# Two-layer hybrid trunk: per-block roots and transposed scaled blocks in the prologue

## The reference

```python
def rmsnorm(x, g):
    xf = x.astype(jnp.float32)
    y = xf * lax.rsqrt(jnp.mean(xf * xf, axis=-1, keepdims=True) + EPS)
    return (y * g.astype(jnp.float32)).astype(x.dtype)

def even_mixer(h, cos, sin, w_in, conv_w, q_g, k_g, w_out):
    p = h @ w_in
    sc, q, k, v, iq, ik, iw = jnp.split(p, EVEN_SPLIT, axis=-1)
    ...
    q = apply_partial_rope(rmsnorm(q.reshape(bsz, s_len, ATT_HEADS, HEAD_DIM), q_g), cos, sin)
    ...
    yb = indexed_sparse_attention(q, k, v, iq, ik, iw * IDX_SCALE, topk)
    return jnp.concatenate([ya, yb], axis=-1) @ w_out

for layer in range(DEPTH):
    x = x + even_mixer(rmsnorm(x, ev_norm[i]), ...)      # layer 0; odd_mixer in layer 1
    x = x + conv_ffn(rmsnorm(x, ffn_norm[layer]), ...)
```

## Time and profile before

| | us |
|---|---|
| median of 3 runs | 2179.6 (2179.0 to 2180.37) |
| span of the profiled execution | 2178.9 |
| TensorE busy | 2073.2 |
| VectorE busy | 1394.8 |
| ScalarE busy | 1099.9 |
| GpSimd busy | 1096.4 |

### The profile page before, as it was taken

How to read it: one execution, slowest core, us unless ns; L and a number is a source line. 1 busy time by engine, 2 the same in 40 slices (tenths; PEclk the granted TensorE clock), 3 DMA queues, 4 the chain that set the end, 5 groups by cost and what they waited for, 6 DMA issues and landing times. The chain is left out here.

```text
span 2178.9 us, 29915 instructions
## 1 busy us (share of the span) xinstructions
PE 2073.2 (95%) x11334; PEld 1008.8 (46%) x11334; DVE 1394.8 (64%) x1998; ACT 1099.9 (50%) x1649; POOL 1096.4 (50%) x840
## 2 busy tenths in 40 slices
PE   6989977889999999999999999989999999999998
PEld 3544435654444444444434444555444444444444
DVE  9788888857775575575544036695867467467552
ACT  6459946644664564554323225443566466455520
POOL 6103333315677767756584023503476766765642
PEclk8999988999999999999999999999999999999999
DMA  4002110002112211212232001101211211221212
GB/s 175 20 1 57 32 31 2 14 13 70 49 58 59 68 49 58 59 49 68 66 105 59 0 20 39 46 5 50 57 49 51 66 58 49 68 59 48 59 40 96
DMA packets 186493, 110.20 MB, mean 51 GB/s; under 512 B 4351, under 2 KB 180902, under 8 KB 186358
## 3 DMA queue, kind: packets, MB, share of 16 engines
q1 hardware_dynamic: 185894, 107.00, 16.5%
q0 software_dynamic: 464, 1.39, 0.2%
HBM read 104.18 MB, written 4.19 MB: 50 GB/s over the span
## 5 line engine op out<-in xcount | busy, mean ns | idle before, releaser
L1229 PE MATMUL ps<-arena 128*128 128x512 f16 x2712 | 594.0, 379 | 3.9 <-DVE ps L2751 2.5
L1229 PEld LDWEIGHTS ps<-arena 128*128 128x128 f16 x2712 | 264.9, 98 | 326.2 <-DVE ps L2751 5.5
L1229 PE MATMUL ps<-h_hi,arena 128*128 128x512 f16 x1216 | 372.1, 381 | 4.7 <-DVE arena L2842 4.2
L782 POOL TENSOR_SCALAR w_scaled<-stage 128x1024 f32<-128x1024 f32 (+4 forms) x82 | 79.4, 969 | 587.7 <-PE ps L1088 415.8
L2760 DVE SCALAR_TENSOR_TENSOR work<-ps,fvec,work 128x1023 f32<-128x1023 f32 (+1 forms) x176 | 221.6, 1279 | 21.8 <-ACT work L1966 18.7
L1229 PE MATMUL ps<-h_lo,arena 128*128 128x512 f16 x608 | 231.8, 381 | 0.0
L1229 PEld LDWEIGHTS ps<-h_hi,arena 128*128 128x128 f16 x1216 | 119.4, 98 | 151.8 <-issue 8.2
L1088 PE MATMUL ps<-arena 128*128 128x512 f16 x708 | 156.4, 383 | 14.0 <-DVE xT L2642 11.7
L836 POOL TENSOR_TENSOR w_scaled<-stage 128x512 f32<-128x512 f32 (+2 forms) x62 | 70.0, 1129 | 193.1 <-ACT stage L1697 192.9
L1697 ACT ACTIVATE stage<-stage 128x2048 f32<-128x2048 f32 (+2 forms) x62 | 104.5, 1686 | 111.7 <-DMA stage<-in_ffn_w_up_dram 95.3
L1088 PE MATMUL ps<-h_hi,arena 128*128 128x512 f16 x576 | 150.3, 382 | 1.7 <-ACT small L1869 1.7
(11 more groups left out here) (370 smaller groups left out, 3868.3 us busy)
## 6 DMA issues: line engine op xcount, KB each, us to landing
stage<-in_ffn_w_up_dram SPq DMA_DIRECT2D x84, 512.0 KB, 3.8
stage<-in_ffn_w_down_dram SPq DMA_DIRECT2D x48, 384.0 KB, 3.2
stage<-in_od_w_in_dram SPq DMA_DIRECT2D x20, 512.0 KB, 3.8
stage<-in_ev_w_in_dram SPq DMA_DIRECT2D x12, 512.0 KB, 3.8
arena<-in_x_dram SPq DMA_DIRECT2D x8, 512.0 KB, 6.7
stage<-in_ffn_w_down_dram SPq DMA_DIRECT2D x16, 256.0 KB, 2.7
out_dram<-arena SPq DMA_DIRECT2D x8, 512.0 KB, 3.5
stage<-in_od_w_out_dram SPq DMA_DIRECT2D x12, 256.0 KB, 2.7
```

The source lines that it names most:

```text
L782: nc.gpsimd.tensor_scalar(scaled, src, W_SCALE, 1.0, ALU.mult, ALU.mult).then_inc(w_parts, 1)
L1229: last = mm(ps[:, bank, :], left, b[:, k, :], start=(fresh and k == 0 and pss == 0), stop=(k == nk - 1 and pss == 2), skip_group_check=True)
```

## The change

The squares of a block are followed at once by its own root and reciprocal (`square_tokens`, `token_root`). Blocks 0 to 3: GpSimd multiplies the tokens of a block in place by their root, between two of its angle steps; TensorE turns the scaled blocks a second time, four blocks to a bank (`h_turn`, 8 tiles); ScalarE makes the high half straight from PSUM with the gain as its scale (`first_high`), and VectorE the low half from PSUM (`first_low`). Blocks 4 to 7 keep the norm on VectorE, with steps m of 8 to 15, its product in `h_second` in the arena. Blocks 0 and 1 are projected together: first both halves of h by the weights' high halves for all 8 tiles, then h's high halves by the weights' low halves. VectorE splits weight tiles 0 to 4, GpSimd 5 to 7. The masks stand behind the weight tiles; `conv_vectors` runs at b = 1. The first four blocks of x and the vectors are issued ahead of the other four. An early root on `small` loads ScalarE's table once.

```diff
-        TW_BY_DVE = (0, 1)
-        TW_BY_POOL = (2, 3, 4, 5, 6, 7)
+        TW_BY_DVE = (0, 1, 2, 3, 4)
+        TW_BY_POOL = (5, 6, 7)
...
-            for b in range(NB):
+            def load_x(b):
                 sp.dma_start(x_tok[:, b, :], t["x"][0, b * P:(b + 1) * P, :]).then_inc(x_landed[b], 16)
+            for b in range(NB // 2):
+                load_x(b)
...
                 sp.dma_start(vrows[at[name]:at[name] + VEC_ROWS[name], :], src).then_inc(vec_landed, 16)
+            for b in range(NB // 2, NB):
+                load_x(b)
             for k in range(KT):
...
+            def normalise(b):
+                pool.wait_ge(x_turned, 2 * b + 2)
+                pool.wait_ge(tok_rstd, b + 1)
+                G.tensor_scalar(x_tok[:, b, :], x_tok[:, b, :], rms8[:, b:b + 1], 1.0, ALU.mult, ALU.mult).then_inc(tok_normed, 1)
             for src, dst in ((2, 4), (3, 5)):
+                if src == 3:
+                    for b in range(NB // 2):
+                        normalise(b)
...
-            norm_lows(0)
...
+            def h_turn(m):
+                hf, k = divmod(m, KT)
+                if k == 0:
+                    pe.wait_ge(tok_normed, NB // 2)
+                if m == 2:
+                    pe.wait_ge(rope_act, 1)
+                if m == 3:
+                    pe.wait_ge(vec_ready, 1)
+                if m >= 4:
+                    pe.wait_ge(h_ready, m - 3)
+                for j in range(4):
+                    last = tr(ps[:, 4 + m % 4, j * P:(j + 1) * P], x_tok[:, 4 * hf + j, k * P:(k + 1) * P], ident[:])
+                last.then_inc(hf_ready, 1)
+            for b in range(6):
+                x_turn(b)
             pe.wait_ge(vec_landed, 16 * 6)
-            tr(ps[:, 5, 0:NVEC], vrows[0:NVEC, :], ident[0:NVEC, 0:NVEC]).then_inc(vec_turned, 1)
+            tr(ps[:, 7, 0:NVEC], vrows[0:NVEC, :], ident[0:NVEC, 0:NVEC]).then_inc(vec_turned, 1)
+            h_turn(0)
+            h_turn(1)
+            x_turn(6)
+            h_turn(2)
+            h_turn(3)
+            x_turn(7)
...
-            spread(0, 0)
-            spread(0, 1)
...
-            tm_project(0)
+            pe.wait_ge(x_evict, 2 * NB)
+            for k in range(KT):
+                pe.wait_ge(tw_hi_made, k + 1)
+                wait_tile(0, 0, k)
+                for b in range(2):
+                    for a in (h_hi, h_lo):
+                        for c0, c1 in ((0, HALF), (HALF, EV_TM)):
+                            mm(pair(b)[:, c0:c1], a[:, k, b * P:(b + 1) * P], tw_hi[:, k, c0:c1], start=(k == 0 and a is h_hi), stop=False)
+                if k < 4:
+                    h_turn(4 + k)
+            pe.wait_ge(h_ready, 7)
+            pe.wait_ge(tok_rstd, NB)
+            for j in range(4):
+                last = tr(ps[:, 6, j * P:(j + 1) * P], rms8[:, 4 + j:5 + j].broadcast_to([P, P]), ident[:])
+            last.then_inc(rstd_spread, 1)
+            for b in range(2):
+                for k in range(KT):
+                    if b == 0:
+                        if k in TW_BY_DVE:
+                            pe.wait_ge(tw_split_dve, TW_BY_DVE.index(k) + 1)
+                        else:
+                            pe.wait_ge(tw_split_pool, TW_BY_POOL.index(k) + 1)
+                    for c0, c1 in ((0, HALF), (HALF, EV_TM)):
+                        last = mm(pair(b)[:, c0:c1], h_hi[:, k, b * P:(b + 1) * P], tw_lo[:, k, c0:c1], start=False, stop=(k == KT - 1))
+                last.then_inc(tm_done, 1)
+            pe.wait_ge(h_ready, 5)
             pe.wait_ge(small_landed, 16 * 8)
             for q in range(4):
                 last = tr(ps[:, 4, q * 4 * FT:(q + 1) * 4 * FT], frows[0:4 * FT, q, :], ident[0:4 * FT, 0:4 * FT])
             last.then_inc(vec_turned, 1)
-            tm_project(1)
             tm_project(2)
             pe.wait_ge(vec_ready, 2)
+            wait_half(0, 1)
             tm_turn(0)
-            wait_half(0, 1)
...
+            def square_tokens(b):
                 act.wait_ge(x_landed[b], 16)
                 if b >= 2:
                     act.wait_ge(sq_ready, b - 1)
-                A(work[:, 2 + b % 2, :], x_tok[:, b, :], ACT.Square, accum_out=rms8[:, b:b + 1]).then_inc(sq_ready, 1)
+                A(work[:, b % 2, :], x_tok[:, b, :], ACT.Square, accum_out=rms8[:, b:b + 1]).then_inc(sq_ready, 1)
+                act.wait_ge(sq_ready, b + 1)
+                A(rms8[:, b:b + 1], rms8[:, b:b + 1], ACT.Sqrt, bias=eps[:, 0:1], scale=1.0 / D).then_inc(tok_rms, 1)
...
+            def first_high(m):
+                hf, k = divmod(m, KT)
+                act.wait_ge(hf_ready, m + 1)
+                if hf:
+                    A(h_hi[:, k, HALF:], h_second[:, m % 4, :], ACT.Copy).then_inc(hhi_ready, 1)
+                else:
+                    A(h_hi[:, k, 0:HALF], ps[:, 4 + m % 4, :], ACT.Copy,
+                      scale=vec[:, VEC_AT["ev_norm"] + k:VEC_AT["ev_norm"] + k + 1]).then_inc(hhi_ready, 1)
             def first_norm():
-                act.wait_ge(sq_ready, NB)
-                A(rms8[:], rms8[:], ACT.Sqrt, bias=eps[:, 0:1], scale=1.0 / D).then_inc(rms_ready, 1)
+                for b in range(6):
+                    square_tokens(b)
                 act.wait_ge(vec_turned, 1)
-                A(vec[:], ps[:, 5, 0:NVEC], ACT.Copy).then_inc(vec_ready, 1)
-                for k in range(3):
+                A(vec[:], ps[:, 7, 0:NVEC], ACT.Copy).then_inc(vec_ready, 1)
+                square_tokens(6)
+                act.wait_ge(vec_ready, 1)
+                first_high(0)
+                first_high(1)
+                square_tokens(7)
+                for k in range(KT):
                     tw_high(k)
-                for m in range(2 * KT):
-                    high(0, m)
-                    if m + 3 < KT:
-                        tw_high(m + 3)
+                    if k + 2 < KT:
+                        first_high(k + 2)
+                for m in range(KT, 2 * KT):
+                    first_high(m)
...
+            def x_out(b):
+                for g in range(2):
+                    n = 2 * b + g
+                    dve.wait_ge(x_turned, n + 1)
+                    V.tensor_copy(xT[:, 4 * g:4 * g + 4, b * P:(b + 1) * P],
+                                  ps[:, n % 4, :].rearrange("p (k m) -> p k m", m=P)).then_inc(x_evict, 1)
+            def token_root(b):
+                dve.wait_ge(tok_rms, b + 1)
+                V.reciprocal(rms8[:, b:b + 1], rms8[:, b:b + 1]).then_inc(tok_rstd, 1)
+            def first_low(m):
+                hf, k = divmod(m, KT)
+                cols = slice(hf * HALF, (hf + 1) * HALF)
+                if m == 0:
+                    dve.wait_ge(vec_ready, 1)
+                dve.wait_ge(hhi_ready, m + 1)
+                if hf:
+                    V.tensor_tensor(h_lo[:, k, cols], h_second[:, m % 4, :], h_hi[:, k, cols], ALU.subtract).then_inc(h_ready, 1)
+                    return
+                V.scalar_tensor_tensor(out=h_lo[:, k, cols], in0=ps[:, 4 + m % 4, :],
+                                       scalar=vec[:, VEC_AT["ev_norm"] + k:VEC_AT["ev_norm"] + k + 1], in1=h_hi[:, k, cols],
+                                       op0=ALU.mult, op1=ALU.subtract).then_inc(h_ready, 1)
...
             dve.wait_ge(dve_filled, 4)
+            for b in range(NB):
+                x_out(b)
+                token_root(b)
+                if b == NB - 2:
+                    first_low(0)
+            for m in range(1, KT):
+                first_low(m)
+            for k in TW_BY_DVE:
+                tw_low(k)
+            level_masks()
             dve.wait_ge(x_evict, 2 * NB)
-            norm(0, VEC_AT["ev_norm"])
+            dve.wait_ge(rstd_spread, NB // 2 + 1)
+            for m in range(KT, 2 * KT):
+                k = m - KT
+                if m >= KT + 4:
+                    dve.wait_ge(h_ready, m - 3)
+                V.scalar_tensor_tensor(out=h_second[:, m % 4, :], in0=xT[:, k, HALF:],
+                                       scalar=vec[:, VEC_AT["ev_norm"] + k:VEC_AT["ev_norm"] + k + 1], in1=ps[:, 6, :],
+                                       op0=ALU.mult, op1=ALU.mult).then_inc(hf_ready, 1)
+                if m > KT:
+                    first_low(m - 1)
+            first_low(2 * KT - 1)
...
                 tm_sum(b)
-                if b == 0:
+                if b == 1:
                     conv_vectors()
```

83 lines of the change are left out of this document (33 added, 50 removed).

## The result

The changed kernel takes **2185.7 us** (median of 5 runs, 2184.8 to 2187.0); the kernel before took 2179.6 in the same comparison (5 runs, 2173.9 to 2180.4). The ratio is 1.0033, 95% interval 1.0022 to 1.0043: slower by 4.8 to 9.4 us. A second comparison of the same two programs gave 1.0039 (1.0026 to 1.0052), medians 2186.6 and 2177.5. The profiled executions last 2178.9 us (before) and 2185.3 us (after), +6.4. The forecast was 2189.2, 9.6 above the median before.

What follows compares the result with a forecast made beforehand. TensorE, busy from 66 to 125 us, was taken as bound by VectorE's chain from the norm's end to block 0's turn. Norm 7.0, filter vectors 1.1 and clock 1.5 sum to 9.6, giving 2189.2 us, range 2182 to 2201.

Steps and rivals of the forecast that it cites:

- The chain that shifts as a piece: From VectorE's last norm subtraction (48.2) to block 0's rotated rows (65.2), everything shifts with the norm's end, forecast +7.0 us.
- Start and first half: Roots, first weight tile and first norm half: first high half at 18.7, TensorE 2.13 per tile, last low half at 28.5.
- Low weight tiles: VectorE's five tiles alternate with GpSimd's instructions, each waiting out the other: 28.5 + 5.0 + 5.7, 39.5 with gaps.
- Masks: 16 small VectorE steps, now behind the weight tiles, cost 5.25 us that nothing hides, to 44.8.
- The filter vectors: Copied on VectorE at b = 1, ready at 66.85 instead of before 65.78, delaying TensorE's turn of block 0 by +1.1 us.
- Clock: TensorE's pause ahead of the turn of block 0 drops its clock to half rate, losing 1.5 us (0 to 2).
- GpSimd's multiplications: Four multiplications of x by the root, price unknown, taken as 1.1 us each like L782, with no delay.
- Rival 1: GpSimd's multiplications by the root take 3.70 each like L963, adding 9.4 us, 2198.6 us; chance 0.28.
- the shift of the norm's end decides: The norm's delay on VectorE, +7.0, passes one for one through TensorE's busy stretch from 66 to 125 us.
- From span to time: Forecast time is the span 2188.5 plus 0.7, as the earlier median 2179.6 stood 0.7 above its span.

Runs made afterwards that it cites:

- Experiments 1: Changed kernel with the 16 mask steps back ahead of the first eviction; 2181.9 us, ratio 1.0018.
- experiment 5: Changed kernel with all eight low weight tiles on VectorE in a row, none on GpSimd; 2184.4 us, ratio 1.0032.
- experiment 4: Kernel before with only the 16 mask steps moved, from ahead of the first eviction to ahead of the norm's second half; 2186.6 us, ratio 1.0042.
- experiment 7: As experiment 6, but TensorE spreads the second half's roots behind weight tile 5 instead of tile 7; 2171.4 us, ratio 0.9973.
- experiment 2: Changed kernel with the filter vectors copied in the round of block 0 again; 2182.9 us, ratio 1.0023.
- experiment 3: Changed kernel with masks ahead of the first eviction and filter vectors in the round of block 0; 2178.1 us, ratio 1.0002.
- experiment 6: As experiment 3, with all eight low weight tiles on VectorE, six between the first half's low halves; 2174.4 us, ratio 0.9984.
- experiment 8: As experiment 7, but TensorE projects block 3 ahead of the turn of block 0; 2175.0 us, ratio 0.9984.
- experiment 11: As experiment 7, but GpSimd starts with the streamed weights only when block 1 is rotated; 2169.2 us, ratio 0.9960.
- experiment 12: As experiment 11, but ScalarE makes the sines ahead of the second norm half and copies block 0 before the last high half; 2165.0 us, ratio 0.9944.

## Why the prediction held, point by point

- **The chain that shifts as a piece.** Right. Norm's end +7.0 forecast, +7.0 measured (55.2); turn of block 0 forecast at 73.9, measured at 73.95; TensorE has no pause in the 59 us that answer to the earlier trace rows:

```profile
74.20:133.20 59.00, 59.00 (x345) 30.34 (x343) 38.31 (x106) 27.38 (x59) 0.00 (x0) 0.97 0.00 1
```

  TensorE's lead of 9.5 us at 46.5 gained nothing, as said. Experiments 1 and 5 moved the turn by about what they moved the norm (5.3 and 5.1 us, 2.7 and 2.4).
- **Start and first half.** Right: first weight tile's high half at 18.8 (18.7 forecast), last low half of the first half at 28.9 (28.5), TensorE's tile with a turn 2.07 (2.13). The granted clock was 1.00 through the 1.66 us pause ahead of 19.0 and behind it.
- **Low weight tiles.** Right, 39.65 against 39.5, and for the reason given: experiment 5. The Trainium skill (SBUF — State Buffer, Who interferes with whom) says that a VectorE instruction with two SBUF inputs contends with a GpSimd instruction that reads SBUF, and calls the shared port pair an exclusive lock. The 2.07 and 10.11 of experiments 4 and 7 beside the 0.29 and 3.50 without GpSimd agree. One size was off: GpSimd's subtraction alone takes 2.0, not the 1.85 of the sum.
- **Masks.** Right here (5.2), but more by their place than the prediction knew. It named no condition for the 5.25; experiment 4 shows 10.0 for the same steps beside GpSimd's work, and my expectation of it (+4.0) was wrong by 2.9 us at the turn.
- **The filter vectors.** The sum was right and two terms in it were not. 7.0 for the norm counted from 65.78, but VectorE's last piece was ready at 65.18, so the norm's delay alone moves the turn by 7.0 - 0.6 = 6.4; the vectors then cost 1.6, not 1.1 (experiment 2). 8.0 or 8.1 either way, 8.2 measured. Experiments 2 and 3, without the vectors, bear this out: the norm is 6.4 and 2.0 later than before, the turn 5.9 and 1.5.
- **Clock.** 1.5 forecast. The distance grows from 8.2 at the turn to 9.7 at the shared matmul in one pair of traces, from 8.1 to 10.5 in the other. Right in kind, between 1.5 and 2.4 in size. The two traces differ in when the clock fell: half clock from about 74.8 to 78.3 in the first, from ahead of the turn at 73.67 to about 78.8 in the second. This term was read from the traces; no experiment was made for it alone.
- **GpSimd's multiplications** cost 1.12, as L782 said. Rival 1, with 0.28 the likeliest of the others, was refuted by the first row. L963's 3.70 is then not the price of the per-partition scalar; the comparison is what is left, and that was not tested.
- **The step that was mis-sized** is the last one, "the shift of the norm's end decides": that all of it reaches the end. Of 9.6 the ratios show 7.2 (4.8 to 9.4) and 8.5 (5.7 to 11.3), all executions together 8.2, the spans 6.4 and 9.2. 9.6 lies just outside the first interval and inside the second, and both pairs of traces lose 1.5 to 2.1 us between the shared matmul and the scores. Named are VectorE's addition near 1145 us (1.1) and the shorter fall of the clock near 1310; behind the scores 1.2 us go in the first pair and none in the second. Neither was in the prediction. What sets them stays open.
- **From span to time.** The 0.7 that the forecast adds comes to the same as 2179.6 + 9.6, and is no error. But the time of one execution is above its own span, by 1.7 to 1.9 us for the kernel before and the changed one (2187.0 and 2185.3) and by 2.0 to 2.2 in experiments 5 to 8, 11 and 12, so the traced execution of before took about 2180.6, 1.0 more than the median.

## What to carry to other kernels

A saving on the busiest engine is worth nothing while another engine's chain releases it: find the piece that ends last at the stage's start, sum the change on that engine in its new order, and look where its small, uncovered steps land. Where VectorE and GpSimd both have two-input work, price each VectorE step at GpSimd's whole instruction, and try giving all of it to VectorE in its gaps, or letting GpSimd start later: eight tiles alone were faster than five shared. And explain a late difference between two kernels only where two traces of each agree on it.

## What the runs showed of the hardware that was not expected

- Short VectorE steps suffer most from GpSimd: 0.29 us became 2.07, and 16 steps went from 5.2 to 10.0 us (experiment 4).
- Six steps of the rotation cost 6.6 us beside GpSimd (10.11 against 3.50). GpSimd's start could be put off by about 12 us (46.60 to 58.35), since it was idle for 98 us afterwards; the collision then moves to block 1, where TensorE did not wait in experiment 11 and waited 1.43 us in experiment 12.
- The same code of some 2027 us took from 2023.8 to 2031.1 us in fourteen traces, and a changed order in the first 60 us changed how GpSimd's and VectorE's instructions met 1000 us later (2.36 against 1.23), whether the kernel was then early or late.
